# An eight-bin expert ring, a last layer product split by token halves, and fill-in matmuls in TensorE's waits

## What is computed

```python
def hybrid_layer(x, ...):
    hn = rmsnorm(x, g_mix); proj = hn @ w_in               # q, k, v, latents, two gates
    ...                                                    # MoBA branch y_a, MLA branch y_b
    merged = sigmoid(gate_a) * (y_a @ w_branch_a) + sigmoid(gate_b) * (y_b @ w_branch_b)
    x = x + merged @ w_out
    x = x + routed_experts(rmsnorm(x, g_ffn), ...)         # top 4 of 32, clamped SwiGLU, 1024 wide
    hp = rmsnorm(x, g_ple)
    return x + sigmoid(hp @ w_ple_gate) * (p_i @ w_ple_proj)

def second_block(x, c, ...):
    c_act = silu(c)
    for l in range(2):
        shift, scale, gate = split(c_act @ w_ada[l] + b_ada[l], 3)
        h = rms_norm(x, g_pre[l]) * (1.0 + scale) + shift
        proj = h @ w_in[l]                                 # 1024 x 3072
        y_a = b_a * causal_conv(c_a * u_a) * silu(gate_a)
        y_p = multiscale_pool(u_p, w_pool[l]) * pool_scale[l] * silu(gate_p)
        y = concat([y_a, y_p]) @ w_out[l]
        x = x + gate * rms_norm(y, g_post[l])
```

## Time and profile before

| | |
|---|---|
| time, median of 3 runs | 1464.35 us (1460.76 to 1464.44) |
| the profiled execution | 1462.8 us, its span 1460.7 us |
| PE busy, share of the span | 1362.1 us, 93% |
| DVE, ACT, POOL busy | 424.0, 274.7, 29.3 us |
| DMA | 498.66 MB, mean 341 GB/s |
| granted TensorE clock, mean | 0.973 of full |

### The profile page before, as it was taken

How to read it: one execution, slowest core, us unless ns; L and a number is a source line. 1 busy time by engine, 2 the same in 40 slices (tenths; PEclk the granted TensorE clock), 3 DMA queues, 4 the chain that set the end, 5 groups by cost and what they waited for, 6 DMA issues and landing times.

```text
span 1460.7 us, 16185 instructions
## 1 busy us (share of the span) xinstructions
PE 1362.1 (93%) x6558; PEld 678.5 (46%) x6558; DVE 424.0 (29%) x655; ACT 274.7 (19%) x392; POOL 29.3 (2%) x46
## 2 busy tenths in 40 slices
PE   8999999999999999989899899999999988997997
PEld 4446644433433333333333333333333336996996
DVE  2344224311211211112112111121112126775773
ACT  2133313010110101101101011011011114532531
POOL 2100100000000000000000000000000000000000
PEclk9999999799999999999999999999999999899899
DMA  9992375799999999999999999999999995355330
GB/s 327 386 332 86 125 285 215 305 409 428 428 429 428 428 429 429 428 429 429 428 428 429 428 428 429 428 428 429 429 427 430 429 406 191 113 176 180 115 117 29
DMA packets 76968, 498.66 MB, mean 341 GB/s; under 512 B 7095, under 2 KB 8586, under 8 KB 52362
## 3 DMA queue, kind: packets, MB, share of 16 engines
q1 hardware_dynamic: 75802, 496.06, 83.1%
q0 software_dynamic: 704, 2.10, 0.4%
q10 hardware_dynamic: 432, 0.07, 0.0%
HBM read 497.06 MB, written 1.05 MB: 341 GB/s over the span
## 4 chain that ended last, share of the span: by engine, by line
PE 57%; DMA 30%; issue 8%; DVE 4%; ACT 1%; POOL 0%; DVEq 0%; SPq 0%; POOLq 0%; ACTq 0%
DMA ring<-in_w_gate_up_dram 30%; PE ps L1569 27%; PE ps L1336 7%; PE ps L1668 3%; PE ps L1670 3%; PE ps L1669 3%; PE ps L1563 2%; PE ps L1501 2%; PE ps L1485 2%; PE ps L1346 1%; PE ps L1550 1%; PE ps L1315 1%; PE ps L1632 1%; PE ps L1573 1%; ACT arena L662 1%
## 5 line engine op out<-in xcount | busy, mean ns | idle before, releaser
L1569 PE MATMUL ps<-ring,arena 128*64 128x512 f32 x3072 | 699.3, 606 | 39.4 <-DMA ring<-in_w_gate_up_dram 26.1
L1569 PEld LDWEIGHTS ps<-ring,arena 128*64 128x64 f32 x3072 | 213.4, 139 | 489.8 <-issue 400.7
L1095 DVE TENSOR_SCALAR arena<-ps 128x512 f32<-128x512 f32 x32 | 22.1, 691 | 350.5 <-PE ps L1569 350.5
L655 ACT ACTIVATE arena<-arena 128x512 f32<-128x512 f32 x32 | 20.2, 630 | 506.4 <-DVE arena L1095 506.4
L1336 PE MATMUL ps<-ring,HT 128*128 128x512 f32 (+1 forms) x256 | 111.3, 586 | 1.3 <-ACT HT L568 1.0
L1670 PE MATMUL ps<-arena_highs,w_low 128*128 128x256 f32 x384 | 109.2, 284 | 0.0
L1056 DVE TENSOR_SCALAR esel<-const 128x128 fp32r<-128x128 f32 x49 | 12.6, 285 | 282.5 <-ACT arena L666 145.1
L666 ACT COPY arena<-ps 64x512 f32<-64x512 f32 x64 | 37.1, 580 | 243.0 <-PE ps L1569 242.7
L1074 DVE TENSOR_TENSOR X<-X,ps 128x1024 f32<-128x1024 f32 x34 | 41.4, 1217 | 126.4 <-PE ps L1563 126.4
L1668 PE MATMUL ps<-arena_highs,ring_highs 128*128 128x256 f32 x256 | 72.8, 284 | 1.5 <-DVE HT_r L1133 1.5
L1670 PEld LDWEIGHTS ps<-arena_highs,w_low 128*128 128x128 f32 x384 | 73.9, 193 | 0.0
(11 more groups left out here) (237 smaller groups left out, 1226.8 us busy)
## 6 DMA issues: line engine op xcount, KB each, us to landing
ring<-in_w_gate_up_dram SPq DMA_DIRECT2D x128, 2048.0 KB, 24.3
ring<-in_w_down_dram SPq DMA_DIRECT2D x64, 2048.0 KB, 21.4
ring<-in_w_in_dram SPq DMA_DIRECT2D x38, 1024.0 KB, 7.3
ring<-in_w_ada_dram SPq DMA_DIRECT2D x24, 1024.0 KB, 13.2
ring<-in_w_out_dram SPq DMA_DIRECT2D x12, 1024.0 KB, 6.3
ring<-in_w_ple_gate_dram SPq DMA_DIRECT2D x4, 1024.0 KB, 23.2
ring<-in_w_branch_a_dram SPq DMA_DIRECT2D x2, 1024.0 KB, 9.6
ring<-in_w_branch_b_dram SPq DMA_DIRECT2D x2, 1024.0 KB, 9.6
```

Of the source, the lines that this page charges most:

```text
L1569: last = T.matmul(ps[at:at + CAP, bank, :], lhsT, w(g), start=False, stop=stop)
```

## The change

- **Ring.** `BINS = 8`: six bins in `ring` as before, and two more of 16 KB a partition in `arena` (`more_bins`). Loads take the bins in turn, so four experts (`QUADS`, 24 loads) make one turn of SP's and PE's loops instead of one and two. The first two loads of expert 1 go to the new bins right behind the last chunk of the first stage (they wait for `y_done`); then come the six of expert 0. The first chunks of the last stage wait for the use of the load eight places back instead of six.
- **Tiles moved.** To free the two arena pieces, the bias rows go to HN, the router's scratch, `tmp`, `yslot`, `glu` to `hidT`, `pin`, `pT` and the rows of `ada` for layer 1 go elsewhere. The bias loads wait for `yTb`. The pads and `inv_windows` are set by POOL after the experts.
- **Adaptive columns of layer 1.** `mod_sums(1)` stands between the last two `scatter`, `mod_columns(1)` on DVE behind the last `add_scattered`.
- **Layer heads.** The squares and the norm are taken by half. DVE writes `rdiag[h]`, a 128x128 diagonal of the norm, in place of the scaled X; PE multiplies X by it in 16 plain float32 matmuls in place of 16 transposes.
- **Layer ends.** The second part of y runs for h and then g. ACT and DVE finish X for half 0 (and, in layer 0, its norm for the next layer) ahead of half 1.
- **Fill-in matmuls.** `keep_busy(bank, n)` issues n float32 matmuls of 128x128 by 512 columns on constants: 2 ahead of the last `count`, 2 ahead of the first gather, 2 behind it, 5 at the head of layer 0 and 3 at the head of layer 1.

```diff
+BINS = 8
+QUADS = E // 4
+PER_QUAD = 4 * GROUPS
+        more_bins = [view(32, 2 * SLOT, "p (a b) -> p a b", a=2), view(56, 2 * SLOT, "p (a b) -> p a b", a=2)]
+        def bin2(s):
+            b = s % BINS
+            return ring[:, 2 * b:2 * b + 2, :] if b < SLOTS // 2 else more_bins[b - SLOTS // 2]
@@ sync
-            expert(0, phase1_left)
-            ada_moved(1)
-            with sp.Fori(0, E - 1) as before_e:
-                expert(before_e + 1, lambda q: sp.wait_ge(s["chunk_used2"], before_e * GROUPS + (q + 1)))
+            sp.wait_ge(s["y_done"], 2)
+            for k in range(GROUPS, BINS):
+                load(1, k)
+            for k in range(PER_QUAD):
+                if k < GROUPS:
+                    phase1_left(k)
+                elif k >= BINS:
+                    sp.wait_ge(s["chunk_used2"], k - BINS + 1)
+                if k < GROUPS or k >= BINS:
+                    load(k // GROUPS, k)
+                if k == GROUPS:
+                    ada_moved(1)
+            with sp.Fori(0, QUADS - 1) as i:
+                quad(i * 4 + 4, lambda k: sp.wait_ge(s["chunk_used2"], i * PER_QUAD + (PER_QUAD + k - BINS + 1)))
-                    sp.wait_ge(s["chunk_used2"], extra * (E * GROUPS) + ((E - 1) * GROUPS + n // 2 + 1))
+                    sp.wait_ge(s["chunk_used2"], extra * (E * GROUPS) + (E * GROUPS - BINS + n // 2 + 1))
@@ gpsimd
+            pool.wait_ge(s["w_highs"], 1)
+            for z, n in ((U, PAD), (Z, 2), (WA, PAD), (WB, PAD)):
+                G.memset(z[:, :, 0:n], 0.0).then_inc(s["pads_set"], 1)
             pool.dma_start(invw, t["inv_windows"]).then_inc(s["inv_in"], 16)
@@ scalar
+            def sum_of_x(l, h):
+                act.wait_ge(s["x_ready"], 2 * l + h + 1)
+                if l + h:
+                    act.wait_ge(s["l_sums"], 2 * l + h)
+                A.activation(conv, X[:, h, :].rearrange("p (a b) -> p a b", a=4), ACT.Square,
+                             accum_out=st[:, 2 + h:3 + h]).then_inc(s["l_sums"], 1)
+                act.wait_ge(s["l_yhalf"], l + 1)
+                for h in range(HALVES):
+                    for g in range(2):
+                        p = filledL(act, l, f"y{g}") if h else UL[f"y{g}"][0]
+                        ...
+                    if l + 1 < LAYERS:
+                        sum_of_x(l + 1, h)
@@ vector
+            dve.wait_ge(s["mod1_full"], 1)
+            mod_columns(1, 5, s["mod1_moved"], 1)
+            def norm_half(l, h):
+                dve.wait_ge(s["l_sums"], l * 2 + h + 1)
+                mean_square(2 + h)
+                power()
+                V.tensor_scalar(rdiag[h], ident, st[:, 2 + h:3 + h], None, ALU.mult).then_inc(s["l_rdiag"], 1)
-                for h in range(HALVES):
-                    V.tensor_scalar(HN[:, h, :], X[:, h, :], st[:, h:h + 1], None, ALU.mult).then_inc(s["l_hn"], 1)
+                for h in range(HALVES):
+                    weigh(0, h)
+                    dve.wait_ge(s["l_ysum"], l * 4 + 2 * h + 2)
+                    lrun(V.tensor_tensor(st[:, h:h + 1], st[:, 8 + 2 * h:9 + 2 * h], st[:, 9 + 2 * h:10 + 2 * h], ALU.add))
+                    ljoin()
+                    mean_square(h)
+                    weigh(1, h)
+                    power()
+                    ...
                     V.scalar_tensor_tensor(X[:, h, :], YG[:, h, :], st[:, h:h + 1], X[:, h, :], ALU.mult, ALU.add
                                            ).then_inc(s["x_ready"], 1)
+                    if l + 1 < LAYERS:
+                        norm_half(l + 1, h)
@@ tensor
+            def keep_busy(bank, n):
+                for _ in range(n):
+                    T.matmul(ps[:, bank, :], ident, const[:, 0:512], start=True, stop=True)
             ada_part(1, 11)
+            keep_busy(2, 2)
             pe.wait_ge(s["mask_done"], 2)
+            keep_busy(2, 2)
             pe.wait_ge(s["tok_highs"], HALVES)
             pe.wait_ge(s["ada_out"], 8)
+            keep_busy(5, 2)
             pe.wait_ge(s["bias_ready"], 2)
-            with pe.Fori(0, extra * PAIRS + PAIRS) as i:
+            with pe.Fori(0, extra * QUADS + QUADS) as i:
+                pair_of_experts(i * 2, 0, loaded)
+                pair_of_experts(i * 2 + 1, 2 * GROUPS, loaded)
                 scatter(h)
+                if h == 0:
+                    mod_sums(1, 5, s["mod1_full"])
-                pe.wait_ge(s["l_hn"], l * 2 + 2)
-                for j in range(2):
-                    p = lfree(f"hT{j}")
-                    features(p, lambda k, h: HN[:, h, (4 * j + k) * P:(4 * j + k + 1) * P]).then_inc(fullL[p], 1)
+                keep_busy(2 * lfree("hT1"), 3 if l else 5)
+                for h in range(HALVES):
+                    pe.wait_ge(s["l_rdiag"], l * 2 + h + 1)
+                    for j in range(2):
+                        p = UL[f"hT{j}"][0] if h else lfree(f"hT{j}")
+                        for k in range(4):
+                            last = T.matmul(flat(p, P, k * S + h * P), X[:, h, (4 * j + k) * P:(4 * j + k + 1) * P],
+                                            rdiag[h], start=True, stop=True)
+                        if h:
+                            last.then_inc(fullL[p], 1)
+                for h in range(HALVES):
+                    for g in range(2):
+                        last = y_part(1, g, h)
+                    if not h:
+                        last.then_inc(s["l_yhalf"], 1)
```

More of the change, by code:

```diff
@@ L205, in build @@
         PL, SG, T1, UA = [view(45 + 4 * i, D) for i in range(4)]
+        rdiag = [U[:, h, PAD:PAD + P] for h in range(HALVES)]
         Z = arena[:, 61 * 256:61 * 256 + 4 * (S + 2)].rearrange("p (a b) -> p a b", a=4)
@@ L242, in build @@
         ring1 = [sem(f"ring1_{i}") for i in range(SLOTS1)]
-        ring2 = [sem(f"ring2_{i}") for i in range(GROUPS)]
+        ring2 = [sem(f"ring2_{i}") for i in range(BINS)]
         ring3 = [sem(f"ring3_{i}") for i in range(SLOTS3)]
@@ L449, in _, with load, quad @@
                     sp.dma_start(wukv, t["w_ukv"][0]).then_inc(s["wukv_in"], 16)
[L451 to L460, removed]
+            def load(e, s):
+                q, two = s % GROUPS, bin2(s)
+                if q < 4:
+                    src = gu_v[ds(e, 1), q].rearrange("e p k n -> (e p) k n")
+                    sp.dma_start(two, src).then_inc(ring2[s % BINS], 16)
+                else:
+                    src = dn_v[ds(e, 1), q - 4].rearrange("e p j n -> (e p) j n")
+                    sp.dma_start(two.rearrange("p a (b n) -> p (a b) n", b=2), src).then_inc(ring2[s % BINS], 16)
+            def quad(e, used):
+                for s in range(PER_QUAD):
+                    used(s)
+                    load(e + s // GROUPS, s)
             def phase1_left(q):
@@ L1194, in y_split @@
                     V.tensor_tensor(low, y, high.bitcast(fp32), ALU.subtract).then_inc(s["y_lows"], 1)
-                dve.wait_ge(s["l_sums"], l * 2 + 2)
-                V.tensor_scalar(st[:, 0:2], st[:, 0:2], 1.0 / D, EPS, ALU.mult, ALU.add).then_inc(s["pow_in"], 1)
-                power()
-                for h in range(HALVES):
-                    V.tensor_scalar(HN[:, h, :], X[:, h, :], st[:, h:h + 1], None, ALU.mult).then_inc(s["l_hn"], 1)
                 for j in range(2):
@@ L1353, in ada_parts, with mod_sums @@
                     ada_part(l, i)
-            def mod_sums(l, p, full):
+            def mod_sums(l, bank, done):
                 pe.wait_ge(s["ada_in"], 256 * (l + 1))
                 for r in range(4):
-                    last = T.matmul(ps[:, 2 * p, 0:24], ada_mods[l][0:24, r, :],
+                    last = T.matmul(ps[:, bank, 0:24], ada_mods[l][0:24, r, :],
                                     ident[0:24, 0:24].rearrange("p (c j) -> p j c", c=4), start=r == 0, stop=r == 3)
-                last.then_inc(full[p], 1)
+                last.then_inc(done, 1)
             for gi in range(4):
```

150 lines of the change are left out of this document (76 added, 74 removed).

## The result

| | before | after |
|---|---|---|
| median | 1462.55 us (1459.0 to 1464.44, 4 runs) | 1438.53 us (1436.47 to 1441.46, 4 runs) |
| ratio, 95% interval | | 0.984 [0.9824, 0.9856] |
| the profiled execution, its span | 1462.8, 1460.7 us | 1436.58, 1434.2 us |
| granted clock, mean | 0.973 | 0.990 |
| DMA | 498.66 MB, 341 GB/s | 498.71 MB, 348 GB/s |

The change is faster by 1.6%, and the predicted 1441.9 us is 3.4 us too high. The forecast took its 22.5 us from a median of 1464.35 us, three of these four runs; between the medians above lie 24.0 us. The same kernel gave 0.984 again in e0 and 0.9843 in e8.

The account below looks back on a forecast made before the run. The experts' steady load stream was taken as the bound, with PE behind it. Gains of 9.8 + 5.2 + 2.4 + 3.2 + 1.9 = 22.5 us gave 1441.9 us from the 1464.35 median; range 1435 to 1451 for 8 in 10.

Parts of the forecast that it names:

- What bounds the kernel: Experts' stage: a steady transfer stream at 4.893 us a load, its end set by its start and the loads left.
- the two bins: Experts' stage: two loads leave the stream and fill an idle DMA hole of 11 us; 9.8 us less.
- (c): Rival: extra loads miss the hole, or the stream doesn't set the end; 9.8 us back, 1451.7 us; chance 0.08.
- (d): Rival: loads that also write the arena slow the stream; slower than before, 1469 us at 3%; chance 0.04.
- Start of the stream: Ahead of the experts: fill-ins hold the clock, so the stream starts at 268.1 instead of 273.35; 5.2 us less.
- (a): Rival: the clock doesn't hold ahead of the experts, the stream starts 1.9 us late; 1449.0 us; chance 0.17.
- Head of layer 0: Norm by halves and plain products bring layer 0's first columns 1.4 us earlier; 2.4 us with the clock.
- Its clock: Fill-ins hold the clock at the layer heads: 1.0 us, half of 2.0, in layer 0; 0.8 us in layer 1.
- Head of layer 1: Half 0 ready early brings layer 1's first columns 2.4 us earlier; 3.2 us with the clock.
- The end: End of the kernel: X of half 0 no longer stands before half 1's, and one square pass goes; 1.9 us less.
- The edits at nothing: Moved ada sums and columns, late chunks, pads, inverse windows, y's new order, small DVE steps: counted at no time.
- better bounds: Both layer heads, if plain products hold the clock where transposes would not: 2.2 us more gain, 1439.7 us.

Follow-up runs that it names:

- e0: The changed kernel again, unaltered, on the same chip as the three that followed; 1439.83 us, ratio 0.984.
- e8: The changed kernel again, unaltered, in one later series with two other kernels, five executions each; 1439.18 us, ratio 0.9843.
- e1: The changed kernel with six bins in place of eight, all else kept; 1447.8 us, ratio 0.99.
- e3: The changed kernel without the three pairs of fill-in matmuls around the first gather; 1443.58 us, ratio 0.9872.
- e9: The changed kernel with more fill-ins, in the column gaps of both layers and between layer 1's halves, a rerun of e7; 1436.81 us, ratio 0.9835.
- e10: The changed kernel without any fill-in matmuls, ahead of the experts or at the layer heads; 1446.95 us, ratio 0.9898.
- e2: The changed kernel with the two extra loads issued in turn behind the first six instead of ahead of them; 1443.2 us, ratio 0.987.
- e5: The changed kernel with DVE scaling X by halves and 16 transposes in place of the diagonal and plain products; 1441.61 us, ratio 0.9852.
- e4: The changed kernel without the fill-in matmuls at the heads of layers 0 and 1; 1442.98 us, ratio 0.987.
- e7: The changed kernel with two more fill-ins behind each layer's products and one between layer 1's halves; 1436.74 us, ratio 0.9829.
- e6: The changed kernel with the second part of y in the old order, output half outside and token half inside; 1445.13 us, ratio 0.9882.

## Why the prediction was right, and where its terms were off

**What bounds the kernel, the two bins: right.** 10.08 us against 9.8, and in e1 10.3 against after; the plateau and the 4.894 us a load did not move, and the landing came at 1163.32 against "near 1164". The first transfer in the chain came four experts later, not five. Rivals (c) and (d) are out by these rows.

**Start of the stream: right, 0.8 too small.** 5.97 against 5.2. The up to 1 us that I allowed for the loop's registers had no row behind it, and it was not there: PE had used the first bin early enough, and the floor of SP's small moves, 267.3, set the start. e3 puts 5.1 of it down to the clock; rival (a) is out, since the clock stood at 1.00 from 250 to 275. That the clock would hold I took from one old stretch, with PE busy 4.41 of 7.80 us. The outcome was right and that reading weak: ahead of the fall at 254.7 PE was busy 2.30 of 3.40 us, a larger share, and ahead of e9's fall in the last expert 1.96 of 3.40. What the runs show is that these six fill-ins went with a clock at 1.00 from 250 to 275 in all ten profiled executions that have them, and that it fell there in the three without (before, e3, e10). The price of (a) was not tried: with the clock low and no fill-ins the first load comes at 272.52 (e10), near the 273.35 of before, and no run had both fill-ins and a low clock there.

**The last expert: a term that I did not have.** Before, the clock fell over the last expert's down product:

```profile
1187.49 8.28 PE L1569 MATMUL ps<-ring,arena 128*64 128x512 f32 x32 [0.25 <-ACT arena L662]
```

In after it stayed up, and the product took 7.1 us. That is 1.3 us of luck: the clock also falls now and then in the middle of the experts, in every kernel, for 3.4 us, and on the path that costs up to half its length. Of the 13 profiled executions six met such a fall behind the last landing (before, e1, e2, e3, e5, e9) and lost 1.2 to 1.7.

**Head of layer 0: right.** 1.45 us against 1.4. **Its clock: mis-sized by its nature.** I counted half of 2.0 us. What happened is nearly all or nothing: 1.75 in after, 0.2 in e0 and e8, where the clock fell at the column gap and cost 1.5. The mean of the three is 0.7, and half of 2.0 is true of none.

**Head of layer 1: 2.4 us predicted, 3.67 measured.** The mechanism was right; what I mis-sized is the walk from PE's stop, 8.1 us where 7.0 were measured (and before it was 10.7, not 10.5). I let half 0's chain end 1.2 us after the stop, and half 1's squares start no earlier than before. ACT had done with half 0 and begun to square one part of half 1 at 1321.73, before PE stopped at 1322.38, and DVE wrote half 0's diagonal by 1322.96. X of half 1 began 2.2 us after the stop, and its products followed without the extra hand-overs that I had added. PE idled 1.5 us between the halves' products, not 2.7. **Its clock: 0.8 predicted, 0.19 measured.** The fill-ins ahead of the products don't reach the gap at which it falls (e4: worth nothing in its profiled execution); with fill-ins behind them it stayed up (e7, e9: 1.5 to 1.6 us).

**The end: right.** 2.05 us against 1.9; e6 gives 0.8 of it back.

**The edits at nothing** cost nothing that a row shows: 0.05 us lie between the scatter and the embedding's gate. What the Trainium skill states of transposes (TensorE: Matmul & The Clock Gate, Part 4: PE-mode transpose), by which both heads would be near their better bounds, gave 1439.7, nearer to the result than my sum. But its mechanism is not shown to have brought it there: the clock fell at gaps behind plain products as behind transposes (e0, e5). Nor did the old row on which I had this trace agree tell the two apart: right behind the transposes the plain products, too, ran for 4.0 us at 0.50.

Of the 26.5 us between the two profiled spans, 22.5 were in the sum. The rest, in the order of the ledger, is 0.77 + 0.28 + 1.29 + 0.05 + 0.05 + 0.75 + 1.27 - 0.61 + 0.15 = 4.0, of which the clock's places in the last expert and the layers make 1.4 and the structure 2.6. By the medians of the three series of this kernel (1438.5, 1439.8, 1439.2) the forecast is 2.1 to 3.4 us high.

## To carry to other kernels

Where a stream of loads at a constant rate ends a stage, count its loads and find when it starts; a buffer more is worth the idle DMA time that its load can fill, and the same buffer filled later is worth half. Work of constants on PE pays ahead of such a start, where all that it saves reaches the end, and at a later gap only, in these runs, where it lies inside the gap at which the clock falls. Between dependent halves, issue the matmuls so that one half is whole early: its chain on the other engines then hides behind the products of the other.

## What the runs showed of the hardware

The clock's first rise came at 7.5 to 8.9 us of the span in eight of 13 executions and at 13.3 to 14.1 in five, whatever the kernel, and the late one costs 2.1 us at the start of the experts. Within the experts each of the 13 shows five to nine single falls of 3.4 us, at places that differ between executions of the same code. PE works through the fall; what stands ahead of it is a pause of PE. Windows of e9, ahead of its fall at 1171.70 in the last expert, and of after, over the same pause and what follows:

```profile
1168.20:1171.60 3.40, 1.96 (x15) 1.53 (x16) 2.74 (x4) 0.88 (x2) 0.00 (x0) 1.00 0.96 405
```

```profile
1168.20:1171.60 3.40, 1.96 (x14) 1.47 (x15) 2.66 (x4) 0.80 (x2) 0.00 (x0) 1.00 0.96 407
1171.70:1175.10 3.40, 3.40 (x18) 1.15 (x16) 0.00 (x0) 0.00 (x0) 0.00 (x0) 1.00 1.01 392
```

PE did the same in both, and the clock fell in one. What picks the pause behind which it falls is not shown. With the gaps of the columns they make up the 4 to 5 us between executions of one kernel, as much as the smaller terms of this change; only positions in the trace, taken from one point to the next, tell such terms apart. What sets the moment of the first rise was not settled.
